# Two attention layers: gates applied inside the attention, the output projection streamed 512 wide and joined to the next norm

## What is computed

```python
def even_layer(x, norm, w_in, gq_a, gk_a, rpb, gq_b, gk_b, w_out, ang_row, ang_col):
    h = rmsnorm_2(x, norm)
    qa, ka, va, qb, kb, vb, gate = _split(h @ w_in, SPLIT_E)
    ...
    oa = neighbourhood_attention(qa, ka, va, rpb)        # 8 heads x 64
    ob = attend_blocks(qb, kb, vb, D_HEAD ** -0.5)       # 8 heads x 64
    o = jnp.concatenate([oa.reshape(B, S, -1), ob.reshape(B, S, -1)], -1) * jax.nn.silu(gate)
    return o @ w_out

def odd_layer(...):
    ...
    oc = attend_blocks(qc, kc, v_c, (C_NOPE + C_ROPE) ** -0.5)
    od = diff_attend_blocks(...)
    od = rmsnorm_2(od, g_sub_d) * (1.0 - lam_init)
    o = jnp.concatenate([oc.reshape(B, S, -1), od.reshape(B, S, -1)], -1) * jax.nn.silu(gate)
    return o @ w_out

x = x + even_layer(x, ...)
x = x + odd_layer(x, ...)
```

## Time and profile before

| | us |
|---|---|
| median of 3 runs | 3324.02 |
| lowest and highest | 3318.54, 3324.17 |
| the profiled execution, its own time | 3324.29 |
| its span, first to last instruction | 3322.7 |
| mean granted TensorE clock, share of full speed | 0.958 |
| busy: TensorE, VectorE, ScalarE, GpSimd | 3024.8, 1652.8, 1174.7, 966.3 |

### The profile page before, as it was taken

One profiled execution on the slowest core, in us unless ns is written; L12 is line 12 of the kernel. 1 busy time (PEld: TensorE's weight loads), 2 busy tenths in 40 slices (PEclk: granted clock), 3 DMA queues, 4 the chain that ended last, 5 costly groups with the idle time before them and its releaser, 6 DMA issues.

```text
span 3322.7 us, 51498 instructions
## 1 busy us (share of the span) xinstructions
PE 3024.8 (91%) x18916; PEld 2646.7 (80%) x18916; DVE 1652.8 (50%) x3095; ACT 1174.7 (35%) x2163; POOL 966.3 (29%) x629
## 2 busy tenths in 40 slices
PE   5898986999999999998999999979598989999969
PEld 4587954777888888788999778968596989988869
DVE  2699724614323322312046568861313938878871
ACT  2311135424222211313122457740322426667640
POOL 1123111242222235552235023311231544432211
PEclk9899997999999999999999999989799999999989
DMA  2122231331111113342395442411235852221311
GB/s 97 57 95 101 79 108 38 95 121 64 48 47 50 44 57 117 115 136 89 108 214 192 101 92 55 133 77 51 80 115 181 223 155 65 56 71 49 116 77 51
DMA packets 220498, 317.22 MB, mean 95 GB/s; under 512 B 80743, under 2 KB 166631, under 8 KB 217143
## 3 DMA queue, kind: packets, MB, share of 16 engines
q1 hardware_dynamic: 185190, 268.90, 27.1%
q10 hardware_dynamic: 33360, 39.98, 3.5%
q0 software_dynamic: 1792, 6.29, 0.7%
HBM read 221.56 MB, written 93.57 MB: 95 GB/s over the span
## 4 chain that ended last, share of the span: by engine, by line
PE 69%; DVE 8%; ACT 3%; issue 2%; POOL 1%; DMA 1%; POOLq 0%; DVEq 0%; ACTq 0%; SPq 0%; PEldq 0%
PE psum L2268 15%; PE psum L506 14%; PE psum L2471 7%; PE psum L1083 6%; PE psum L1052 6%; PE psum L2222 6%; PE psum L1063 5%; PE psum L767 2%; PE psum L744 2%; PE psum L2019 2%; DVE arena L2869 2%; PE psum L756 1%; DVE arena L2858 1%; PE psum L1098 1%; PE psum L3207 1%
## 5 line engine op out<-in xcount | busy, mean ns | idle before, releaser
L2268 PE MATMUL psum<-parts_ffn 128*128 128x512 f32 x2112 | 482.6, 391 | 3.6 <-DVE parts_ffn L2169 3.6
L2268 PEld LDWEIGHTS psum<-parts_ffn 128*128 128x128 f32 x2112 | 398.9, 189 | 87.0 <-issue 2.2
L506 PE MATMUL psum<-parts_even,parts_ffn 128*128 128x256 f32 x2496 | 306.8, 286 | 5.2 <-DVE parts_ffn L2605 4.0
L506 PEld LDWEIGHTS psum<-parts_even,parts_ffn 128*128 128x128 f32 x2496 | 304.6, 195 | 5.9 <-DVE parts_ffn L2605 4.5
L506 PE MATMUL psum<-parts_odd 128*128 128x248 f32 x2304 | 276.0, 283 | 19.5 <-ACT arena L543 14.6
L506 PEld LDWEIGHTS psum<-parts_odd 128*128 128x128 f32 x2304 | 273.3, 193 | 21.5 <-ACT arena L543 15.6
L2338 DVE SCALAR_TENSOR_TENSOR arena<-psum,arena 128x1023 f32<-128x1023 f32 x88 | 112.9, 1283 | 329.8 <-ACT arena L2322 323.6
L543 ACT ACTIVATE arena<-psum 128x256 f32<-128x256 f32 (+1 forms) x232 | 87.4, 382 | 492.0 <-PE psum L506 486.4
L435 PE MATMUL psum<-parts_mixer 128*128 128x512 f32 x912 | 211.7, 395 | 10.7 <-ACTq L444 10.7
L435 PEld LDWEIGHTS psum<-parts_mixer 128*128 128x128 f32 x912 | 174.3, 191 | 48.3 <-ACTq L444 7.6
L1125 ACT ACTIVATE both<-psum 128x512 fp32r<-128x512 f32 x256 | 139.9, 596 | 109.2 <-PE psum L1063 108.8
(11 more groups left out here) (345 smaller groups left out, 5857.2 us busy)
## 6 DMA issues: line engine op xcount, KB each, us to landing
arena<-ffn_up_b SPq DMA_DIRECT2D x44, 512.0 KB, 3.3
arena<-ffn_down_k SPq DMA_DIRECT2D x44, 512.0 KB, 3.6
arena<-x SPq DMA_DIRECT2D x10, 2048.0 KB, 8.8
arena<-w_in_e SPq DMA_DIRECT2D x13, 1024.0 KB, 6.7
e_tokens<-arena ACTq DMA_DIRECT2D x26, 512.0 KB, 3.2
arena<-w_in_o SPq DMA_DIRECT2D x12, 992.0 KB, 5.6
o_tokens<-arena ACTq DMA_DIRECT2D x24, 496.0 KB, 3.0
arena<-w_in_f SPq DMA_DIRECT2D x19, 512.0 KB, 3.3
```

The source lines that it names most:

```text
L506: last = pe.matmul(self.bank(t), self.hT[:, a, k, t * P:(t + 1) * P], self.weights.parts[:, self.weights.slot(s), b, k, :], start=(k, a, b ...
L2268: last = pe.matmul(self.core.psum[:, 4 * u + 2 * s + h, :], parts[:, s, a, k, :], self.hT[:, b, k, h * HALF:(h + 1) * HALF], start=(k, a, ...
```

## The change

The gates go through Silu when ScalarE takes them out of PSUM, in tok3b and tok4b (`gates_from`). axial and latent get the gate rows of their half in SBUF and multiply by them in `finish`: one product of 128x128 becomes two of 128x64 with a scale and a gate. The other half's rows (near's and combine's) are multiplied by their gates on GpSimd (`gate_first`). A new class `GatedBranches` gives `OutNorm` the transposes of both halves, and `OutNorm` takes the place of `GateTranspose` and `OutProjectSplit` in both layers: for out3 without the gain after the projection but with the next norm, hT and a hand-over into tok4a like the one from down to tok3a; for out4 without any norm. `Handover` and norm4 go. The semaphores of the even layer are retired in out3, behind GpSimd's split of weight slice 8, and those of out3 in step 9 of tok4b. The output weights are laid out by rows instead of by column blocks. The classes `Handover`, `GateTranspose` and `OutProjectSplit` are deleted.

```diff
@@ ProjectTokens.take_out
-        act.activation(self.stage[:, h, j, :], self.bank(t), ACT.Copy).then_inc(self.act_out, 1)
+        plain = self.width if self.gates_from == self.blocks * self.width else min(max(self.gates_from - (i * 2 + s) * self.width, 0), self.width)
+        for a, b, function in ((0, plain, ACT.Copy), (plain, self.width, ACT.Silu)):
+            if a < b:
+                last = act.activation(self.stage[:, h, j, a:b], self.bank(t)[:, a:b], function)
+        last.then_inc(self.act_out, 1)
@@ WideAttention.vector
+        hold(dve, self.gate_ready)
...
+            if self.gate is not None:
+                columns = self.heads[s](i, dv)
+                for j in range(2):
+                    last = dve.scalar_tensor_tensor(out=self.out_sb[:, t + j, columns], in0=ps[:, 7, j * dv:(j + 1) * dv],
+                                                    scalar=self.inv[:, n % 4 + j:n % 4 + j + 1], in1=self.gate[:, t + j, columns],
+                                                    op0=ALU.mult, op1=ALU.mult)
+                last.then_inc(self.finished, 1)
+                return
@@ class GatedBranches (new)
+        self.done = [(self.low_out, 16)]
+        self.x_after = [(self.turned, 16)]
+        self.plan = [range(4)] + [range(2 * n + 2, 2 * n + 4) for n in range(1, 7)]
...
+    def gate_first(self, pool, after):
+        pool.wait_ge(self.gate_loaded, 32)
+        for k in range(4):
+            hold(pool, after(k))
+            x = self.first[:, :, k * P:(k + 1) * P]
+            pool.tensor_tensor(x, x, self.first_gate[:, :, k * P:(k + 1) * P], ALU.mult).then_inc(self.gated, 1)
+
+    def ready(self, pe, k):
+        pe.wait_ge(self.low_out, k + 1)
...
+    def turn(self, pe, n):
+        b, h, c = n // 8, n // 4 % 2, n % 4
+        if b == 0:
+            pe.wait_ge(self.gated, c + 1)
+        if n == 3:
+            hold(pe, self.second_done)
+        if n >= 4:
+            pe.wait_ge(self.low_out, n - 3)
...
@@ OutNorm.sync, gpsimd, opening
-                hold(sp, self.branches.dsa.results_out + self.branches.lru_split)
+                hold(sp, self.branches.x_after)
...
+            if n in self.before_split:
+                self.before_split[n](pool)
...
-            if n == self.K:
+            if n == self.K and self.retire is not None:
                 self.retire.clear(pool)
...
+                for turn in branches.plan[3 * t + n]:
+                    branches.turn(pe, turn)
                 if t == 0:
+                    branches.ready(pe, n)
                     pe.wait_ge(self.w_low, n + 1)
                 self.multiply(pe, n, t)
-        self.retire.leave(pe)
+        for turn in branches.plan[6]:
+            branches.turn(pe, turn)
+        if self.retire is not None:
+            self.retire.leave(pe)
         hold(pe, branches.done)
@@ OutNorm.turn_second, scalar, vector
-        for k in range(KT):
+        for k in range(KT) if t is None else {1: range(4), 3: range(4, KT)}.get(t, ()):
...
+            if self.post_gain is None:
+                dve.wait_ge(self.x_loaded[t // 4], 16)
+                dve.wait_ge(self.summed, t + 1)
+                dve.tensor_tensor(self.xs[:, t], self.xs[:, t], self.sum_of(t), ALU.add).then_inc(self.drained, 1)
+                return
@@ build, even layer
+        rest.gates_from = 512
...
-        turn_a = GateTranspose(core, "turn3a", ...), turn_b = GateTranspose(core, "turn3b", ...)
-        out3 = OutProjectSplit(core, "out3", a["w_out_e"], catT, x2, x3, residual, ...)
-        st = add(Handover(core, arrived, opened, st.done))
+        branches = GatedBranches(core, "even_branches", near_rows, near_gate, axial_rows, axial_gate, axial.done, hT)
+        retired = Retire(core, arrived, opened, of_even, [])
+        out3 = OutNorm(core, "out3", branches, a["w_out_e"], x2, x3, None, col["norm_o_2"], hT, raw, wring, residual, ys, None, ..., retired)
+        add(Part(sync=... load axial_gate after st_e.done)), add(axial)
+        add(Part(sync=... load near_rows after near.done)), add(Part(sync=... load near_gate after near.done))
+        add(Part(gpsimd=... gate_first)), add(out3)
@@ build, odd layer
-        norm = add(NormTranspose(core, "norm4", x3, col["norm_o_2"], hT, start_o, [], xs=residual))
+        rest.gates_from = 1952 - 1488
+        project.after, project.second_half, project.between = out3.half_done, out3.done[1:], out3.turn_second
+        out3.open_by_scalar, out3.next_load = project.start_scalar, project.weights.load_first
+        gone = add(Retire(core, arrived, opened, of_out3, []))
+        st = add(ProjectAndPrepare(rest, prep, pool_pieces={9: gone.clear}))
...
+        branches_o = GatedBranches(core, "odd_branches", diff_rows, diff_gate, latent_rows, latent_gate, latent.done, catT)
+        out4 = OutNorm(core, "out4", branches_o, a["w_out_o"], x3, out, None, None, None, raw, wring, residual, None, None, None, diff.done, None)
+        out4.before_split = {2: lambda pool: branches_o.gate_first(pool, lambda k: [(combine.result, k + 2)])}
```

More of the change, by code:

```diff
@@ L1896, in __init__ @@
         self.done = [(self.low_out, 10)]
+        self.x_after = dsa.results_out + self.lru_split
+        self.plan = [range(2 * n, 2 * n + 2) for n in range(5)] + [(), ()]
+    def ready(self, pe, k):
+        if k == 0:
+            hold(pe, self.lru_split)
     def split_recurrence(self, pool):
@@ L2132, in part @@
         def part(act, h, k):
+            if (h, k) == (0, 0) and self.open_by_scalar is not None:
+                hold(act, self.retire.done)
+                self.open_by_scalar(act)
             source, high, _ = self.parts_of(h, k)
@@ L2170, in part @@
                                      op1=ALU.subtract).then_inc(self.low_out, 1)
+        if self.col_gain is None:
+            for t in range(TT):
+                drain(dve, t)
+            return
         self.order(dve, drain, finish, part)
@@ L3557, in build @@
         core.back_to(start)
-        place = core.top
-        turn_b_xs = shaped(core.arena[:, place + 8 * S:place + 12 * S], (TT, HALF))
+        place = (start + 7) // 8 * 8
+        near_top = after_near
+        block4 = lambda at: shaped(core.arena[:, at:at + 4 * S], (TT, HALF))
+        near_rows, near_gate, axial_rows = (block4(place + 4 * S * n) for n in range(3))
+        gate_at, ring_at = core.words - 4 * S, place + 12 * S
+        eps_at = ring_at + 6 * S
+        raw_at = eps_at + 3 * TT
@@ L3564, in build @@
         near.ahead = axial.start_gpsimd
-        core.open_parts("parts_even_out")
-        catT = core.take_parts(2, KT, S)
-        core.top = place
-        residual = core.take(TT, D)
-        core.top = place
-        turn_a = GateTranspose(core, "turn3a", [(attended[:, 0:512], 0)], e_tok[:, 2304:2816], catT, axial.done, near.done, near.done)
-        turn_b = GateTranspose(core, "turn3b", [(attended[:, 512:1024], 4)], e_tok[:, 2816:3328], catT, axial.done + turn_a.done,
-                               axial.done, near.done, x_ready=axial.done)
@@ L3573, in build @@
-        out3 = OutProjectSplit(core, "out3", a["w_out_e"], catT, x2, x3, residual, turn_a.done + turn_b.done, turn_a.done,
-                               near.done, axial.done)
-        add(axial)
-        for load in (turn_a.load_x, turn_a.load_gate, turn_b.load_gate, out3.weights.load_first, out3.load_x):
-            add(Part(sync=load))
-        add(turn_a), add(turn_b)
-        st = add(out3)
-        st = add(Handover(core, arrived, opened, st.done))
+        core.open_parts("parts_odd")
@@ new lines, in build @@
+        hT = core.take_parts(2, KT, S)
+        parts_base = core.parts_top
+        of_even = list(core.used)
+        branches = GatedBranches(core, "even_branches", near_rows, near_gate, axial_rows, axial_gate, axial.done, hT)
+        retired = Retire(core, arrived, opened, of_even, [])
+        wring = [shaped(core.placed(f"out3_ring{n}", ring_at + 2 * D * n, 2 * D, F32R), (2, D)) for n in range(3)]
+        raw = shaped(core.arena[:, raw_at:raw_at + 2 * D], (2, D))
+        ys = [core.arena[:, at + D * t:at + D * (t + 1)] for at in (place + 8 * S, gate_at) for t in range(4)]
@@ new lines, in build @@
+        residual = shaped(core.arena[:, place:place + 8 * S], (TT, D))
+        out3 = OutNorm(core, "out3", branches, a["w_out_e"], x2, x3, None, col["norm_o_2"], hT, raw, wring, residual, ys, None,
+                       core.arena[:, eps_at:eps_at + 2 * TT + 1], near.done + st.done, retired)
+        add(Part(sync=lambda sp: branches_e.load_rows(sp, axial_gate, e_tok[:, 2816:3328], st_e.done, axial_gate_loaded)))
+        add(axial)
+        add(Part(sync=lambda sp: branches_e.load_rows(sp, near_rows, attended_e[:, 0:512], near.done, branches_e.first_loaded)))
```

336 lines of the change are left out of this document (119 added, 217 removed).

## The result

The changed kernel takes 3242.2 us in the median (3240.0 to 3245.7, 4 runs), the kernel before 3322.1 (3318.5 to 3324.2, 4 runs). The ratio is 0.9762, with a 95% interval from 0.9745 to 0.9778: 80 us faster. The forecast was 3245, with a range from 3228 to 3267.

A forecast was written before the change was run, and what follows sets the result against it. TensorE was taken as the bound, 69% of the chain that ended last. 3324.3 - 58.7 (even layer) - 27.2 (odd layer) + 0.5 + 5.1 (Silu tables) + 0.4 (gate) = 3244.4, stated as 3245 us, range 3228 to 3267.

The forecast's parts named there:

- the two large terms: Gains from the last attention matmul on: even layer through out3 into tok4a 58.7 us, odd layer to the end 27.2.
- Stream, transposes, first product: Output projection, each layer: first product at +2.2, 384 matmuls 90.2 us, twelve transpose groups 5.2, exposed last groups 1.6.
- Weights: Output projection: GpSimd's weight split (3.1 us) covered by only two products (2.8) at three places, 0.5 each, 1.5 together.
- the residual: Its 4.2 MB load sits in SP's queue ahead of weight slice 5; slices 5 to 7 just late, 1.5 us (0 to 10).
- the starved stream: Rival: the residual holds up SP's queue longer; at half rate each layer loses some 11 us more, 3267; chance 0.11.
- Clears: out3: Retire's 81 semaphore clears on GpSimd after slice 8's split, about 6.1 us, make slice 9's split 3.8 late.
- Hand-over to tok4a: out3's last product to tok4a's full stream, modelled on down to tok3a without its 4.25 wait for scaled rows: 28.7 us.
- The rival that nothing overlaps: Fused norm: tok4a's first tiles wait for the second half too, some 15 us more, 3260; chance 0.08.
- Table switches: Silu evictions in tok3b and tok4b: 22 loads, 28.2 us of ScalarE, costing 0.5 and 5.1; full-cost rival 3267, chance 0.11.
- Gate in the normalisation: Attentions: VectorE's product becomes two of half width, at most 0.28 us more, hidden by 0.58 slack; 0.4 for round starts.
- The upward terms listed (2, 6 and 8): Upward parts of the forecast's own range: matmul time 226 to 238 ns +2, Silu +6, the residual +8.
- the hold-up beside GpSimd: Rival: GpSimd splits hold up the attentions' gated product; with the full 4.3 us, 238 us more, 3483; chance 0.02.

## Why the prediction was right, term by term

The total was 3 us off, and that is not the luck of one sum: the two large terms hold by themselves, 58.7 against 59.1 and 27.2 against 27.1. Within the first some errors cancel, and that part is luck: out3 took 2.1 more than the 107.0 predicted, and the hand-over 2.7 less.

- **Stream, transposes, first product.** The odd layer shows it cleanly: 103.4 us against the predicted 102.2. Its parts: first product after 1.9 (predicted 2.2); 36 + 348 matmuls at 237 ns, 91.1 (90.2); twelve groups 5.3 (5.2); the exposed pair 1.57 (1.6).
- **Weights, a mis-sized term.** I wrote 0.5 at each of three places, 1.5 together. It is 0.88 at four places, 3.5: GpSimd's subtraction takes 2.39 us in out3 and out4, not the 2.00 of the earlier trace rows, and the last slice of the second half waits as well. The error is made up by the residual, 1.5 (0 to 10), which cost nothing: its two loads landed in 11.1 us in the median, and no slice from 5 to 7 was waited for longer than the others. That rival, the starved stream, did not occur; a slower residual was not tried, so how much room it had is open.
- **Clears.** 3.8 predicted; 3.32 of wait and 1.4 of clock behind it, 4.9 when moved away. The clock was missing from that step, and its own terms (6.1 + 3.1 - 5.5) make 3.7. The mechanism (a drain that is too short to hide 81 clears) was right.
- **Hand-over to tok4a.** 28.7 predicted from the last product to the full stream, 26.0 measured: 6.8 to the first product (7.6) and 19.2 from there (21.1). The 4.25 wait vanished as argued. The rival that nothing overlaps would have been 7.2, not 15: it was too dear, since the transposes and half of the tiles are done by then.
- **Table switches.** 5.6 predicted, 3.2 measured in the mean, 2.3 of it in eviction waits, all in tok4b; tok3b's cost nothing that shows. Here the Trainium skill ("ScalarE: Activation LUTs", section "What ACT_TABLE_LOAD costs") would have added a drain to each switch. Both kernels' traces show the next activation 0.01 us behind the load, and 12 further loads added 1.1 us, so its rule to batch by set is sound but worth little where ScalarE waits anyway.
- **Gate in the normalisation.** 0.4 predicted; axial is unchanged to 0.01 us and latent longer by 0.5. The Trainium skill ("SBUF — State Buffer", section "SBUF: two separate sides") limits the blocking to two SBUF inputs or a two-port mode, and the traces agree in both directions: 15 products held up with two SBUF inputs, none of the 18 pairs that read PSUM beside GpSimd.
- **The end.** 5.6 predicted from the last product to the end of the kernel, 4.4 measured.
- **Not in the sum:** tok3a and tok3b together are 2.5 us shorter. Changed kernels that are alike there took 332.0 to 334.8, which makes scatter likely; of the kernel before, with 335.0, there is one profile. This is in part why the profiled span came out below the forecast although the terms agree.
- **The range.** The upward terms listed (2, 6 and 8) lead to 3260, not 3257; the final range of 3228 to 3267 is not touched by it.

One question the sum never asked: it priced the transposes as work wherever they stand, which was right, but not what their mixing with products brings. Only the run with all transposes first showed that this part of the change is worth nothing, and that the opening's gain is the waits for the gate products and two bursts at a low clock. Nor did it ask why eight gate products of 0.69 us kept TensorE waiting for 15.7: the hold-up beside GpSimd, which it named as a rival for the new product, was already in the kernel before and made some 12 us of each layer's wait.

## What to carry to other kernels

Take elementwise work off a boundary between stages by folding it into an instruction that runs anyway and reads PSUM; an instruction of its own between SBUF operands can cost many times its length if GpSimd is at work (0.29 us became up to 2.15 here). When such an instruction is slow, look first at what GpSimd does beside it: moving that may be the smaller change. Price an overlap by the wait that it covers, not by the work that it moves: one here was worth nothing, its twin 7 us. And look what stands behind a semaphore wait or a clear on the engine that feeds TensorE; two small edits there took 12 us off the two output stages, and the median fell by another 0.5%.

## What was not expected of the hardware

The same idle time does not always cost the same clock. Before tok3b's first head transposes TensorE waits 3.18 us both in the kernel with the clears later and in that with all transposes first, whose code there is the same. In the first the 13 transposes then take 1.64 us, in the second 3.04:

```profile
1721.13 1.64 PE L2837 MATMUL psum<-arena 128*128 128x128 f32 x13 [3.18 <-POOL arena L2823]
```

```profile
1719.55 3.04 PE L2837 MATMUL psum<-arena 128*128 128x128 f32 x13 [3.18 <-POOL arena L2823]
```

The window over the second's transposes has a granted clock of 0.56, near the lower of the two levels (1.2 of 2.4 GHz); the first's has 1.00. What decides it no run here shows; the Trainium skill ("TensorE: Matmul & The Clock Gate", section "What's actually happening") says that one kernel can see a different count of slow matmuls from run to run, and that much agrees. It is one source of the few us by which single runs differ.

GpSimd's subtraction of a weight slice, the same instruction on the same shape, takes 2.00 us in all 16 slices of out1 and 2.34 to 2.41 in all of out3 and out4. The operands lie at other addresses, and VectorE and ScalarE do other work beside it; which of these it is was not tried. The 0.39 us between the two are as much as the waits on a slice grew, from 0.50 in out1 to 0.88.
